# Merge stage of a three-branch mixer kernel: the LRU branch first, its first operands prepared in the stage before

## The chip, the cores and the metric

One Trainium2 chip, one core, one launch. The metric is device time in microseconds: the median of the runs of the whole kernel, about 2.9 ms.

## The reference, cut to what matters

One step of a backbone layer over 1152 tokens (128 of context, 1024 latent), width 1024, all in fp32. One input projection feeds three recurrent mixers: gated linear attention (GLA), a diagonal state space (S5) and a gated linear recurrence (LRU, width 1536). Then:

```python
ys   = gelu(s5_outputs)                                 # (T, 1024)
y_s5 = ys * sigmoid(ys @ s5_w_glu)                      # "GLU"
g_gla, g_s5, g_lru = split(sigmoid(gates), 3)
merged = (g_gla * (y_gla @ w_br_gla) + g_s5 * (y_s5 @ w_br_s5)
          + g_lru * (y_lru @ w_br_lru))
out = merged @ w_out
x = layer_norm(ALPHA * x + gate1 * out); then a squared-ReLU MLP and a second layer_norm
```

`gate1` and the other modulation vectors are silu(c) times rows of `w_ada`.

## The kernel before, in words

The program is a chain of stages. Each ends in `core.end_stage()` (line 143): the semaphores of the stage are cleared and all engines meet at a barrier. The two stages that matter are `s5_and_gates` (line 1504) and `merge_and_mlp` (line 2316).

An fp32 product is made of three TensorE passes: each operand is split in a high part (fp32r) and a low part (operand minus high part), and hi*hi, hi*lo and lo*hi are accumulated. A weight unit is 128 x 1024; it is loaded to `raw`, the high part goes to `hi`, the low part to `lo`, with two buffers of each (`Stream`, line 157). In the GLU, LRU, GLA and S5 parts of the merge GpSimd makes both parts (`Stream.split`, lines 194 and 197). A unit of activations ("tile", 128 channels x 1152 tokens) is read into one of four buffers `yin`; ScalarE copies it to a slot of `yhi` (`fill_act`, line 2478, the copy is line 2496) and VectorE subtracts to a slot of `ylo` (`fill_dve`, line 2506). There are 12 slots.

**The state-space stage.** For n = 0 to 15 (groups of 4 state-space groups) TensorE makes input products, lag blocks and outputs (`outputs`, line 1879, lines 1889 and 1891), and between them 3 or 4 "bands" of 24 matmuls of the gate projection (`band`, line 1818, line 1831). `outputs(n - 1)` comes in iteration n, so the last outputs come in iteration 16 (`LAST`), behind the last two bands. ScalarE applies the sigmoid to each band (`evac_gate`, 1981) and stores the gate tile, sets the chunk-boundary states that `outputs` waits for (`resets`, 2011 to 2015, semaphore `hn_done`), and applies gelu to the outputs (`evac_y`, 2024). SyncE, in each iteration and in this order: kernel blocks to DRAM (8 transfers, 1742 and 1744), outputs of the group before to `y_d` (8 transfers, 1753), the state weights `wia` back (8 transfers, 1761). After the loop it stores the final states (1763) and waits for all of it.

**The merge.** TensorE runs four parts in turn, with the loop `for ph in range(OUT)` at line 2666: GLU (8 output tiles m, 8 input tiles k each), LRU (8 m, 12 k), GLA (8, 8) and S5 (8, 8); for each (m, k) nine matmuls of 128x128 by 128x384 (`tile_product`, 2643, line 2662), 2592 in all. Output tile m uses banks 0 to 2 (m even) or 3 to 5 (m odd). The semaphore `used` counts (m, k) pairs, `filled` the slots filled. GLU's inputs are the tiles of `y_d`, which lie in DRAM with the time index inside the group and are turned by the strided read of both fill operations (`turned`). GLU's banks go through a sigmoid on ScalarE (2779) and two VectorE operations over a whole tile (2952, 2953), and the result is stored to `y_s5`. LRU, GLA and S5 multiply the banks by the gate tile into `x1` (`gated`, 2995, 2998, 2999). VectorE also makes 32 modulation vectors, two products each with a row of `w_ada` (`dots`, 2965): two per m in LRU, one per m in GLA and S5. There is one row buffer, so a row is loaded after the products with the row before. Slots of the next part are filled while the last tile m = 7 of the part before uses them up; on VectorE the fills stand behind the `dots` of m = 7 and before its `gated`. SyncE issues weights, gate tiles and rows in one written order (2510 to 2560).

After the four parts, `w_out`, the norms and the MLP follow (line 2695); nothing there is changed.

Of the kernel before, what the change touches and what calls it, by code (L numbers as in the profile page):

```python
# [15 lines left out]
P = 128  # L16
# [5 lines left out]
NB = 3  # L22
# [12 lines left out]
LBLK = 12  # L35
CONV = 4
# [70 lines left out]
class Early:  # L107
    COLS = 4 * T + HEADS * DK + 4 * HEADS + NPAIR + T // 2 + 2 * UW

    def __init__(self, nc, ctx):  # L110
# [9 lines left out]
        self.hi, self.lo = sb("gla_hi", [P, UW], F32R), sb("gla_lo", [P, UW], F32R)  # L120

# [1382 lines left out]
def s5_and_gates(core, hhi, hlo, lam):  # L1504

    nc, dram = core.nc, core.dram
    with ExitStack() as ctx:
# [53 lines left out]
        wt = [sb(f"wt{c}", [P, G4 * P]) for c in "ri"]  # L1561
        wtmp = sb("wtmp", [P, G4 * P])
        win = sb("win", [P, 2 * G4, P])
# [8 lines left out]
        def table_buffer(s):  # L1572
# [15 lines left out]
        kst = [sb(f"kst{s}", [P, KW]) for s in range(2)]  # L1588
        sb("kst_pad", [P, 2 * (G4 - 1) * KW])
# [4 lines left out]
         scan_done, rot_done, fin_s, hn_done, kd_out, y_out0, y_out1, fin_out, const_done) = (  # L1594
# [4 lines left out]
                "kd_out", "y_out0", "y_out1", "fin_out", "const_done"))  # L1599
# [6 lines left out]
        tab_in, y_out = [tab_in0, tab_in1], [y_out0, y_out1]  # L1606
# [38 lines left out]
        with nc.Block() as block:  # L1645
            @block.sync
            def _(sync):
# [77 lines left out]
                for n in range(LAST + 1):  # L1725
# [21 lines left out]
                    if n:  # L1747

                        sync.wait_ge(item_free, Y_ITEM[n - 1] + 1 + 1)
                        m = n - 1  # L1750
                        for t in range(SCH):
                            dst = dram["y_d"][m * G4 * S5I:(m + 1) * G4 * S5I].rearrange("(g i) t c -> i g t c", i=S5I)[:, :, t, :]
                            sync.dma_start(dst, yb[m % 2][t * S5I:(t + 1) * S5I]).then_inc(y_out[m % 2], 16)
                    if n < NBT:
# [7 lines left out]
                sync.wait_ge(fin_s, 2 * NBT)  # L1762
                sync.dma_start(dram["new_s5"], fins[:]).then_inc(fin_out, 16)
                sync.wait_ge(fin_out, 16)
                for s in range(2):
                    sync.wait_ge(y_out[s], 128 * (NBT // 2))
                    sync.wait_ge(gate_out[s], 16 * (UNITS_G // 2))

            @block.gpsimd
            def _(pool):  # L1770
# [35 lines left out]
                for n in range(LAST + 1):  # L1806
# [7 lines left out]
                    splits(bands(n, 3))  # L1814

            @block.tensor
            def _(pe):
# [61 lines left out]
                def outputs(n):  # L1879
# [4 lines left out]
                    pe.wait_ge(hn_done, 2 * n + 2)  # L1884
                    for x in range(2):
                        bk = item(Y_ITEM[n] + x)
# [6 lines left out]
                        mm.then_inc(item_done, 1)  # L1893
# [37 lines left out]
            def _(act):  # L1931
# [132 lines left out]
                for n in range(LAST + 1):  # L2064
# [16 lines left out]
                    if n:  # L2081
                        evac_y(n - 1)
                    for b in bands(n, 3):
                        evac_gate(b)

            @block.vector
            def _(dve):
# [228 lines left out]
def merge_and_mlp(core, mod, x1):  # L2316
# [6 lines left out]
    with ExitStack() as ctx:  # L2323
        ctx.callback(core.end_stage)

# [3 lines left out]
        def sem(name):  # L2329
# [4 lines left out]
        GLU, LRU, GLA_, S5_, OUT = range(5)  # L2334
        ORDER = [list(range(8)), [8, 9, 10, 11, 0, 1, 2, 3, 4, 5, 6, 7], [8, 9, 10, 11, 0, 1, 2, 3],
                 [4, 5, 6, 7, 8, 9, 10, 11], list(range(8))]
        USED = [0, 64, 160, 224, 288]
        FILL = [0, 8, 20, 28, 36]
        UNIT = [0, 8, 24, 32, 40]
        S = Stream(core, "mrg")  # L2340
        yhi = sb("yhi", [P, LBLK, T], F32R)
        ylo = sb("ylo", [P, LBLK, T], F32R)
# [44 lines left out]

        WHI = [S.hi[0][:], S.hi[1][:]] + [yhi[:, n, 0:UW] for n in (8, 9, 10, 11, 0, 1)]
# [65 lines left out]
        for ph, name, off in ((LRU, "y_lru", 1), (GLA_, "y_gla", 2), (S5_, "y_s5", 0)):  # L2454
            for k, slot in enumerate(ORDER[ph]):
                tile = slot if ph == LRU else k
                loads.append((name, tile + off, slot))
# [7 lines left out]
        free_at = ([None] * 4 + [last_use(GLU, s) for s in range(8)] + [last_use(LRU, s) for s in (8, 9, 10, 11, 0, 1, 2, 3)]  # L2465
# [866 lines left out]
```

## Time and profile before

| | |
|---|---|
| median of 3 runs | 2923.47 us (2921.84 to 2925.73) |
| the profiled execution | 2925.48 us, span 2923.6 us |
| PE busy (matmul) | 2776.7 us, 95% of the span |
| DVE, ACT, POOL busy | 1776.7, 1133.3, 939.2 us |
| mean granted clock of TensorE | 0.982 of full speed |
| state-space stage, last band of the gates begins its last matmul | 1483.34 us |
| merge, TensorE's first matmul | 1510.35 us |
| first matmul of `w_out` | 1975.03 us |

The span runs from the first to the last instruction; the execution's own time lies 1.9 us above it. PE is TensorE's matmul side, DVE VectorE, ACT ScalarE, POOL GpSimd, SP SyncE; a q behind an engine's name marks its queue, that is issued transfers, register and semaphore work. L2662 is line 2662 of the kernel. A name is cut to its stem: w_raw, w_hi and w_lo are the weight buffers. The granted clock is given as a share of 2.4 GHz: 1.00 is that, 0.50 is 1.2 GHz.

### The profile page before, as it was taken

To read this page: it belongs to the slowest core of one execution; us is meant where nothing else is said; L and a number is where in the kernel's file an instruction comes from. 1 tells how busy PE (TensorE), PEld (TensorE's weight loads), DVE (VectorE), ACT (ScalarE), POOL (GpSimd) and SP (SyncE) were. 2 spreads that over 40 slices of the span, in tenths; PEclk is the share of its full clock that TensorE was granted. 3 is DMA by queue.
4 is the path that set the end of the run, shared out by engine and by line. 5 is a ranking of instruction groups with operands and counts; after the bars stand their busy time and mean duration, and the time that the engine had idled before them with its cause. 6 is when DMAs were issued, how large, how long until landed. Compare 5 with 4: busy or idle time off the path is not lost. (4 is left out here: it accounts for less than half of the span.)

```text
span 2923.6 us, 41670 instructions
## 1 busy us (share of the span) xinstructions
PE 2776.7 (95%) x16768; PEld 2717.0 (93%) x16768; DVE 1776.7 (61%) x2422; ACT 1133.3 (39%) x1709; POOL 939.2 (32%) x624
## 2 busy tenths in 40 slices
PE   6999999999999998999969999999999999999996
PEld 6999998899999998999969999999899999999996
DVE  7678876454454899999964547778732233223226
ACT  2698995352643323444441101014632211211224
POOL 1344443111211265666523433333112212111223
PEclk9999999999999999999989999999999999999998
DMA  6111112011201444444453536344111111111111
GB/s 230 45 66 55 66 60 62 28 34 44 58 24 42 140 163 145 125 124 123 117 179 118 190 130 224 128 134 140 36 44 44 44 40 42 43 44 44 44 44 65
DMA packets 112716, 257.81 MB, mean 88 GB/s; under 512 B 22496, under 2 KB 56288, under 8 KB 112288
## 3 DMA queue, kind: packets, MB, share of 16 engines
q1 hardware_dynamic: 102464, 214.27, 23.6%
q10 hardware_dynamic: 10080, 41.18, 3.9%
q8 instruction: 117, 1.92, 0.3%
q14 instruction: 55, 0.45, 0.1%
HBM read 199.01 MB, written 56.37 MB: 87 GB/s over the span
## 5 line engine op out<-in xcount | busy, mean ns | idle before, releaser
L153 POOL TENSOR_TENSOR w_lo<-w_raw,w_hi 128x256 fp32r<-128x256 f32 x292 | 348.6, 1224 | 704.5 <-ACT w_hi L205 494.7
L2695 PE MATMUL bank<-yhi,w_hi 128*128 128x384 f32 x1560 | 525.4, 337 | 3.3 <-POOL w_lo L2625 1.8
L2695 PE MATMUL bank<-ylo,w_hi 128*128 128x384 f32 x1560 | 522.0, 335 | 0.0
L2695 PE MATMUL bank<-yhi,w_lo 128*128 128x384 f32 x1560 | 521.9, 335 | 0.0
L2625 POOL TENSOR_TENSOR w_lo<-w_raw,w_hi 128x1024 fp32r<-128x1024 f32 x69 | 169.4, 2456 | 678.4 <-ACT w_hi L2803 678.4
L2662 PE MATMUL bank<-yhi,w_hi 128*128 128x384 f32 x864 | 291.7, 338 | 29.5 <-POOL w_lo L197 24.0
L2695 PEld LDWEIGHTS bank<-yhi,w_hi 128*128 128x128 f32 x1560 | 293.6, 188 | 6.8 <-POOL w_lo L2625 2.5
L2695 PEld LDWEIGHTS bank<-ylo,w_hi 128*128 128x128 f32 x1560 | 293.6, 188 | 1.2 <-issue 0.3
L2695 PEld LDWEIGHTS bank<-yhi,w_lo 128*128 128x128 f32 x1560 | 293.5, 188 | 0.0
L2662 PE MATMUL bank<-ylo,w_hi 128*128 128x384 f32 x864 | 290.5, 336 | 0.0
L2662 PE MATMUL bank<-yhi,w_lo 128*128 128x384 f32 x864 | 290.3, 336 | 0.0
L3114 DVE SCALAR_TENSOR_TENSOR x<-bank,mod,x 128x384 f32<-128x384 f32 (+2 forms) x256 | 126.1, 515 | 242.1 <-PE bank L2695 241.8
L1831 PE MATMUL bank<-hhi,w_hi 128*128 128x384 f32 x744 | 257.9, 347 | 6.6 <-ACT gate L1965 6.6
L1831 PE MATMUL bank<-hhi,w_lo 128*128 128x384 f32 x744 | 251.3, 338 | 0.0
L1831 PE MATMUL bank<-hlo,w_hi 128*128 128x384 f32 x744 | 251.1, 337 | 0.0
L433 PE MATMUL bank<-hhi,w_hi 128*128 128x384 f32 x648 | 218.6, 337 | 13.9 <-DVE hlo L768 10.2
L3103 DVE TENSOR_TENSOR mrg_scr<-gt 128x384 f32<-128x384 f32 x96 | 53.6, 558 | 282.5 <-ACT yhi L2831 282.4
L433 PE MATMUL bank<-hlo,w_hi 128*128 128x384 f32 x648 | 218.0, 336 | 0.0
L433 PE MATMUL bank<-hhi,w_lo 128*128 128x384 f32 x648 | 218.0, 336 | 0.0
L2803 ACT ACTIVATE w_hi<-w_raw 128x1024 fp32r<-128x1024 f32 x69 | 72.6, 1052 | 324.4 <-PE bank L2695 313.6
L2662 PEld LDWEIGHTS bank<-yhi,w_hi 128*128 128x128 f32 x864 | 163.5, 189 | 32.8 <-POOL w_lo L197 24.9
L194 POOL TENSOR_TENSOR w_hi<-w_raw,zero 128x1024 fp32r<-128x1024 f32 (+1 forms) x40 | 77.7, 1943 | 273.0 <-PE bank L2662 176.9
(453 smaller groups left out, 6504.5 us busy)
## 6 DMA issues: line engine op xcount, KB each, us to landing
w_raw<-in_mlp_units SPq DMA_DIRECT2D x64, 512.0 KB, 3.6
w_raw<-in_s_units SPq DMA_DIRECT2D x32, 512.0 KB, 4.6
mrg_scr<-in_w_ada_rows SPq DMA_DIRECT2D x32, 512.0 KB, 3.7
mid_gates<-gate ACTq DMA_DIRECT2D x24, 576.0 KB, 3.6
gt<-mid_gates SPq DMA_DIRECT2D x24, 576.0 KB, 3.9
w_raw<-in_gla_units SPq DMA_DIRECT2D x25, 512.0 KB, 3.7
w_raw<-in_lru_units SPq DMA_DIRECT2D x24, 512.0 KB, 3.7
x<-in_x_t SPq DMA_DIRECT2D x16, 576.0 KB, 9.9
```

The source lines that it names most:

```text
L153: ins = pool.tensor_tensor(lo[:, part], raw[:, part], hi[:, part].bitcast(F32), ALU.subtract)
L194: pool.tensor_tensor(self.hi[par][:, w], self.raw[par][:, w], self.core.zero.to_broadcast([P, width]), ALU.add).then_inc(self.hi_done, 1)
L433: mm = pe.matmul(out, wts[u % 2][:, w], r[:, k, cols], start=(k == 0 and n == 0), stop=(k == KD - 1 and n == 2))
L1831: mm = pe.matmul(out, wts[par][:, w], r[:, k, cols], start=(k == 0 and x == 0), stop=(k == KD - 1 and x == 2))
L2625: pool.tensor_tensor(WLO[SLOT[u]], S.raw[u % 2], WHI[SLOT[u]].bitcast(F32), ALU.subtract).then_inc(S.split_done, 1)
L2662: mm = pe.matmul(out, wt[par][:, w], r[:, slot, cols], start=(k == 0 and n == 0), stop=(k == len(order) - 1 and n == 2))
L2695: mm = pe.matmul(out, wt[SLOT[u]][:, w], r[:, k, band_cols(b)], start=(k == first and y == 0), stop=(k == last and y == 2))
L2803: act.activation(WHI[SLOT[u]], S.raw[u % 2], ACT.Copy).then_inc(S.hi_done, 1)
L3103: st(dve.tensor_tensor(asq, r, r, ALU.mult))
L3114: ins = dve.scalar_tensor_tensor(x1[:, m, c0:c1], core.bank[n % 6][:, c0 - b * BW:c1 - b * BW], mod[:, 5 * KD + m, c:c + 1], x1[:, m, c0:c ...
```

## The change

The merge's order becomes LRU, GLU, GLA, S5, with new slot orders. Buffers `x1` and `yhi`/`ylo` (now one array) are laid out under `hhi`/`hlo` and are given from a class `Merge` with semaphores that live across the barrier. In the state-space stage's last two iterations, the first LRU weight unit, half of the second and two LRU tiles are loaded (the tiles into the dead buffers of the input weights), and split by ScalarE, GpSimd and VectorE; six more LRU tiles are loaded raw into `x1`. The last outputs go to banks 6 and 7, and their gelu and store come in the merge. The final states are stored from ScalarE's queue. The state weights of n = 15 are loaded before the outputs of n = 14 are stored. GLU works by bands with a bank as scratch.

```diff
@@ s5_and_gates, SyncE, iteration n
+                    if n == NBT - 1:
+                        state_weights()
+                        sync.wait_ge(S.split_done, UNITS - 2 + 3)
+                        sync.dma_start(merge.raw[0][:], dram["w_br_lru"][0][:, 0:UW]).then_inc(merge.w_in[0], 16)
+                        sync.wait_ge(item_done, T_ITEM[NBT - 1] + 1 + 1)
+                        sync.wait_ge(w_done, NBT)
+                        for k in range(Merge.LEAD):
+                            sync.dma_start(lead_raw[k], dram["y_lru"][k + 1]).then_inc(merge.y_in[k], 16)
+                        sync.wait_ge(S.split_done, UNITS - 1 + 3)
+                        sync.dma_start(merge.raw[1][:, 0:4 * P], dram["w_br_lru"][0][:, UW:UW + 4 * P]).then_inc(merge.w_in[1], 16)
+                    if n == LAST:
+                        sync.wait_ge(band_done, GATED)
+                        for k in range(Merge.LEAD, KD):
+                            sync.dma_start(merge.x1[:, k, :], dram["y_lru"][k + 1]).then_inc(merge.y_in[k], 16)
+                    elif n:
...
-                sync.wait_ge(fin_s, 2 * NBT)
-                sync.dma_start(dram["new_s5"], fins[:]).then_inc(fin_out, 16)
@@ s5_and_gates, GpSimd, behind its loop
+                pool.wait_ge(merge.w_hi, 1)
+                low_parts(pool, merge.lo[0], merge.raw[0], merge.hi[0]).then_inc(merge.w_lo, 1)
+                pool.wait_ge(merge.w_hi, 2)
+                pool.tensor_tensor(merge.lo[1][:, 0:4 * P], merge.raw[1][:, 0:4 * P], merge.hi[1][:, 0:4 * P].bitcast(F32),
+                                   ALU.subtract).then_inc(merge.w_lo, 1)
@@ s5_and_gates, ScalarE
-                    if n:
+                    if n and n < LAST:
                         evac_y(n - 1)
                     for b in bands(n, 3):
                         evac_gate(b)
+                    if n == NBT - 1:
+                        act.wait_ge(merge.w_in[0], 16)
+                        act.wait_ge(band_done, 3 + NB * (UNITS - 1))
+                        act.activation(merge.hi[0][:], merge.raw[0][:], ACT.Copy).then_inc(merge.w_hi, 1)
+                act.wait_ge(band_done, GATED)
+                for k in range(Merge.LEAD):
+                    act.wait_ge(merge.y_in[k], 16)
+                    act.activation(merge.y[:, k, 0, :], lead_raw[k], ACT.Copy).then_inc(merge.y_hi, 1)
+                act.wait_ge(merge.w_in[1], 16)
+                act.activation(merge.hi[1][:, 0:4 * P], merge.raw[1][:, 0:4 * P], ACT.Copy).then_inc(merge.w_hi, 1)
+                act.wait_ge(fin_s, 2 * NBT)
+                act.dma_start(dram["new_s5"], fins[:]).then_inc(fin_out, 16)
+                act.activation(warm[:], ident[:, 0:1], ACT.Gelu_apprx_tanh)
@@ s5_and_gates, VectorE, behind its loop
+                for k in range(Merge.LEAD):
+                    dve.wait_ge(merge.y_hi, k + 1)
+                    dve.tensor_tensor(merge.y[:, k, 1, :], lead_raw[k], merge.y[:, k, 0, :].bitcast(F32),
+                                      ALU.subtract).then_inc(merge.y_lo, 1)
@@ merge_and_mlp
-        GLU, LRU, GLA_, S5_, OUT = range(5)
+        LRU, GLU, GLA_, S5_, OUT = range(5)
@@ merge_and_mlp, SyncE
+                for f in range(KD, LBLK):
+                    sync.dma_start(yin[f % 4][:], dram["y_lru"][f + 1]).then_inc(yin_in[f % 4], 16)
                 lru_units(1)
+                tile_of("gates", 2 * KD, 0, 0)
+                tile_of("gates", 2 * KD + 1, 0, 1)
+                sync.wait_ge(merge.last_free, 2)
... (8 stores of the last outputs to y_d, then crow and bada)
+                for m in range(5, KD):
+                    lru_units(m)
+                    tile_of("gates", 2 * KD + m, m // 2, m % 2)
+                    for a in (2 * m - 9, 2 * m - 8):
+                        load_row(a, 2 * a)
+                for m in range(2):
+                    tile_unit(GLU, m, m)
+                load_row(7, 14)
+                for m in range(2, KD):
+                    tile_unit(GLU, m, m % 2)
+                    load_row(6 + m, 12 + 2 * m)
+                for m in range(2):
+                    tile_unit(GLA_, m, m)
+                    load_row(14 + m, 28 + 2 * m)
                 for s in range(2):
                     sync.wait_ge(y_out[s], 16 * (KD // 2))
+                for m in range(2):
+                    tile_of("gates", m, 4 * GLA_, m)
+                load_row(16, 32)
+                for m in range(2, KD):
+                    tile_unit(GLA_, m, m % 2)
...
@@ merge_and_mlp, ScalarE
+                act.wait_ge(merge.last_mm, 2)
+                for x in range(2):
+                    act.activation(merge.yb[:, 2 * x:2 * x + 2, :],
+                                   core.bank[LAST_BANK[x]][:, 0:2 * NCH].rearrange("p (g c) -> p g c", c=NCH),
+                                   ACT.Gelu_apprx_tanh).then_inc(merge.last_free, 1)
+                for f in range(Merge.LEAD, LBLK):
+                    fill_act(act, f)
...
+                for f in range(12, 20):
+                    fill_act(act, f)
@@ merge_and_mlp, VectorE
                 for m in range(KD):
-                    dots(2 * m)
-                    dots(2 * m + 1)
+                    if m >= 4:
+                        dots(2 * m - 8)
+                        dots(2 * m - 7)
                     if m == KD - 1:
-                        for n in range(12, 20):
-                            fill_dve(dve, n)
+                        for f in range(12, 20):
+                            fill_dve(dve, f)
                     gated(LRU, m)
```

Fills 12 to 19 are now GLU's turned tiles, 20 to 27 GLA's and 28 to 35 S5's. GpSimd's splits keep their rule (a unit is split when its buffers are free), now in the new order and from the second LRU unit on.

## Rows read from the trace of the kernel before

**Rows 1.** Waits of PE in 1480 to 1980 us: total, times, longest.
```profile
PE bank L2662 <- POOL w_lo L197: 24.0, 3, 21.5
PE bank L2662 <- DVE ylo L2506: 5.5, 7, 1.6
```

**Rows 2.** Timeline around the barrier: start us, us, engine, what, [idle before <-releaser].
```profile
1483.72 0.49 ACT L1981 ACTIVATE gate<-bank 128x384 f32<-128x384 f32 x1 [3.67 <-PE bank L1831]
1485.35 0.21 ACT L2015 ACTIVATE hn<-s_init 64x8 f32<-64x8 f32 x1
1485.66 0.48 PE L1889 MATMUL bank<-ub,wia 128*128 128x144 f32 x2 [1.98 <-DMA wia<-mid_kd]
...
1488.43 0.41 PE L1891 MATMUL bank<-hn,ca1i 128*128 128x144 f32 x2
1489.48 3.63 SPq L1753 DMA_DIRECT2D mid_y_d<-yb  x8
1493.15 0.43 SPq L1763 DMA_DIRECT2D out_new_s<-s_fins  x1
1495.95 0.10 POOL L2602 MEMSET ln_eps<- 128x1 f32 x1 [42.08 <-POOLq L146]
...
1510.35 0.69 PE L2662 MATMUL bank<-yhi,w_hi 128*128 128x384 f32 x1 [21.51 <-POOL w_lo L197]
```

**Rows 3.** Windows: stretch, us, PE, PEld, DVE, ACT, POOL busy, PEclk, DMA, GB/s.
```profile
1496.50:1509.50 13.00, 0.00 (x0) 0.00 (x0) 7.14 (x3) 7.35 (x4) 5.39 (x2) 0.50 0.98 381
1510.30:1526.50 16.20, 14.71 (x63) 13.43 (x63) 16.18 (x6) 12.34 (x7) 7.79 (x2) 0.82 0.76 240
1628.00:1660.00 32.00, 28.20 (x159) 27.16 (x158) 19.80 (x21) 2.91 (x3) 16.06 (x8) 1.00 0.64 231
1660.00:1776.00 116.00, 116.00 (x671) 116.00 (x670) 59.85 (x73) 7.02 (x6) 46.46 (x25) 1.00 0.47 155
1776.00:1804.00 28.00, 25.29 (x136) 24.64 (x135) 23.68 (x29) 5.85 (x5) 9.16 (x5) 0.94 0.69 235
```

**Rows 4.** Timeline of SP's queue, last iterations of the state-space stage.
```profile
1473.98 0.42 SPq L1744 DMA_DIRECT2D mid_kd<-kst  x1
1476.00 3.64 SPq L1753 DMA_DIRECT2D mid_y_d<-yb  x8
```

**Rows 5.** DMA issues: engine queue, count, KB each, median us to landing.
```profile
w_raw<-in_s_units SPq DMA_DIRECT2D x32, 512.0 KB, 4.6
out_new_s<-s_fins SPq DMA_DIRECT2D x1, 64.0 KB, 1.6
```

**Rows 6.** Lines of one source line each: duration in ns, min/median/max.
```profile
L1981 ACT ACT_TABLE_LOAD  x16: 1283/1283/1283, 1055.3 to 1476.0; - x16
L2496 ACT ACTIVATE yhi<-yin x36: 1154/1172/2277, 1500.1 to 1874.4; 128x1152 fp32r<-128x1152 f32 x36
L2506 DVE TENSOR_TENSOR ylo<-yin,yhi x36: 1345/1358/4292, 1502.4 to 1875.6; 128x1152 fp32r<-128x1152 f32 x36
L194 POOL TENSOR_TENSOR w_hi<-w_raw,zero x40: 1041/1894/3706, 1504.0 to 1950.0; 128x1024 fp32r<-128x1024 f32 x32, 128x512 fp32r<-128x512 f32 x8
L197 POOL TENSOR_TENSOR w_lo<-w_raw,w_hi x40: 1287/2493/4129, 1506.3 to 1951.9; 128x1024 fp32r<-128x1024 f32 x32, 128x512 fp32r<-128x512 f32 x8
```

**Rows 7.** The chain that ended last, stretch 1500 to 1800 us: start us, us, what.
```profile
1504.43 2.68 DVE ylo L2506
...
1508.05 2.69 DVE ylo L2506
...
1752.15 1.02 DVE x L2995 x2
...
1756.58 3.73 DMA mrg_scr<-in_w_ada_rows
...
1763.06 14.26 DVE ylo L2506 x5
...
1786.67 6.11 DMA w_raw<-in_w_br_gla
```

More of the change, by code:

```diff
@@ L35 @@
 LBLK = 12
+LAST_BANK = (6, 7)
 CONV = 4
@@ L2324, in merge_and_mlp @@
         ctx.callback(core.end_stage)
+        core.sems += merge.sems
         def sb(name, shape, dt=F32):
@@ L2453, in merge_and_mlp @@
         loads = []
-        for ph, name, off in ((LRU, "y_lru", 1), (GLA_, "y_gla", 2), (S5_, "y_s5", 0)):
+        for ph, name, off in ((LRU, "y_lru", 1), (GLU, "y_d", 0), (GLA_, "y_gla", 2), (S5_, "y_s5", 0)):
             for k, slot in enumerate(ORDER[ph]):
-                tile = slot if ph == LRU else k
-                loads.append((name, tile + off, slot))
+                loads.append((name, k + off, slot))
         def last_use(ph, slot):
@@ new lines, in raw_tile, with fill_act @@
+        def raw_tile(f):
+            if f < KD:
+                return x1[:, f, :]
+            return turned(yin[f % 4]) if loads[f][0] == "y_d" else yin[f % 4][:]
+        def fill_act(act, f, src=None, slot=None):
+            if src is None:
+                src, slot = raw_tile(f), loads[f][2]
+                if f >= 14:
+                    act.wait_ge(filled, f - 1)
+                    issue(act, f + 2)
+                if f < KD:
+                    act.wait_ge(merge.y_in[f], 16)
+                else:
+                    act.wait_ge(yin_in[f % 4], ring(f)[1])
+                if free_at[f] is not None:
+                    act.wait_ge(used, free_at[f])
@@ new lines, in _ @@
+                for t in range(SCH):
+                    dst = dram["y_d"][last * G4 * S5I:(last + 1) * G4 * S5I].rearrange("(g i) t c -> i g t c", i=S5I)[:, :, t, :]
+                    sync.dma_start(dst, merge.yb[t * S5I:(t + 1) * S5I]).then_inc(merge.y_out[last % 2], 16)
+                sync.wait_ge(merge.y_out[0], 128 * (NBT // 2))
+                sync.dma_start(crow, dram["crow"].rearrange("c d -> (c d)").partition_broadcast(P)).then_inc(crow_in, 16)
+                sync.dma_start(bada[:], dram["bada"][:, NMOD1:6 * KD]).then_inc(bada_in, 16)
@@ L3188, in build @@
         mod = ctx.enter_context(nc.sbuf_tensor("mod", [P, 6 * KD, 2], F32))
+        core.weight_buffers(ctx)
+        with ExitStack() as over:
+            merge = Merge(core, over)
         with ExitStack() as hctx:
@@ L3283, in layout @@
     out["s5_init"] = np.ascontiguousarray(st.transpose(1, 3, 0, 2)).reshape(P, 2, GROUPS)
-    order = [LBLK - HG + k for k in range(HG)] + list(range(LBLK - HG))
-    w = f["w_br_lru"][0].reshape(LBLK, P, D)[order].reshape(LBLK * P, D)
-    out["w_br_lru"] = units(w, slice(None))
-    for name in ("w_br_gla", "w_br_s5", "w_out"):
+    for name in ("w_br_lru", "w_br_gla", "w_br_s5", "w_out"):
         out[name] = units(f[name][0], slice(None))
```

273 lines of the change are left out of this document (138 added, 135 removed).

## The prediction

> **What bounds the kernel now.** I read the windows first. In 1660 to 1776 us, inside the LRU part, PE is busy for all of 116.00 us with 671 matmuls, 0.173 us each, at clock 1.00 [rows 3]: the merge runs at TensorE's rate, and only time in which TensorE stands still or runs slow can be won. The waits of PE say where it stands: 21.5 us in one wait for a low part of a weight unit, and 8.0 us in all the rest (2.5 for low parts, 5.5 for filled slots) [rows 1]. The timeline around the barrier shows that wait. The last band is done when its sigmoid starts, at 1483.7. PE waits 1.98 us, makes the last outputs (1485.66 to 1488.84) and then stands 21.51 us, to 1510.35 [rows 2]. In that time the outputs are stored (3.63 us of issue), the final states too, the barrier opens at 1495.95, and from 1496.5 to 1509.5 DMA runs at 381 GB/s with a share of 0.98 [rows 2, 3]: the merge has to load, split and fill before its first matmul.
>
> The merge itself loses in three stretches. A stretch's loss is its length less its matmuls by 0.173. Start, 1510.3 to 1526.5: 16.2 - 63 x 0.173 = 5.3. GLU to LRU: 32.0 - 159 x 0.173 = 4.5. LRU to GLA: 28.0 - 136 x 0.173 = 4.5 [rows 3]. With 1.98 and 21.51 that is 37.8 us which the change can touch. Matmuls, outputs and everything from `w_out` on stay as they are.
>
> **The change, part by part.**
>
> *Step 1, the wait before the last outputs.* The state weights no longer stand behind the store of outputs 14, so the transfer that ended the 1.98 us comes 3.6 us earlier. But ScalarE now has a wait for the first LRU weights in front of the last two sigmoids, and behind those stand the resets that TensorE waits for. SyncE issues the last kernel block by 1474.4 [rows 4]. I put its landing 2 us later (between the 1.6 and 4.6 of [rows 5], nearer the small transfer), then 8 transfers at the pace of the y store, 3.64 us [rows 4]: 1480.0. A 512 KB unit lands 4.6 us after issue in this stage [rows 5]: 1484.6. Then ScalarE makes the high part, about 1.04 us (a 1152-column copy takes 1.17 [rows 6], scaled), and reloads the sigmoid table, 1.28 [rows 6], which the idle time hides today. The first sigmoid begins at 1486.9, the last at 1487.4. From the start of the last sigmoid to the end of the last reset it is 1.84 us [rows 2]: 1489.3. TensorE starts its outputs at 1489.4, 5.7 us after the last band instead of 1.98, and ends them at 1492.6. Bounds: 2 (the weights land before ScalarE is there) to 9 (they come 3 us later, behind gate and state traffic). TensorE's last bands are not held up, since their banks are freed by the bands before.
>
> The Trainium skill's page ScalarE: Activation LUTs, section What ACT_TABLE_LOAD costs, says that a drain of about 1.38 us comes on top of a load of 1283 ns. The row agrees with the load; with that drain in series step 1 would be 7.1 us instead of 5.7.
>
> *Step 2, from the outputs to the merge's first matmul.* Behind the resets ScalarE copies two tiles (2 x 1.17), the half unit (0.5) and issues the final states (0.43): 1492.6. VectorE's two subtractions (1.36 each [rows 6]) and GpSimd's low parts (2.5 and 1.3) end by about 1494. The final states took 1.6 us to land [rows 5], but now six raw tiles of 576 KB, issued from 1485.5 on, are in the DMA engines: 3.5 MB at 381 GB/s is 9 us, to 1495. I take 2.4 us, and for the barrier the 0.77 between landing (1493.58 + 1.6) and 1495.95 [rows 2]. The merge opens at 1495.8, about when it does today: the 4 us saved on the y store go to the new chain. TensorE then needs only the counts that SyncE sets; SyncE's loads today reach full rate 0.55 us behind the barrier [rows 2, 3], so 0.6 us: first matmul 1496.4 instead of 1510.35. The idle is 3.8 us in place of 21.5. Bounds 2.5 (states land in 1.6, no other traffic) and 8 (4.6 for them, and gate stores late).
>
> *Step 3, the start.* Two tiles are ready, 18 matmuls. The clock of 0.82 over 16.2 us is 2.9 us lost at the 1.2 GHz level [rows 3]; the idle is shorter, but [rows 3] also show 0.94 over 28 us (1.7 us) around a wait of only some 2 us, so I keep 2.9 (bounds 0 and 5.3, all of today's loss). Meanwhile ScalarE evacuates the last outputs (0.7, an estimate for twice 288 columns at the rate of [rows 6]) and fills at 1.17 and 1.36 us per tile, faster than the nine matmuls' 1.56. The third tile is ready 3.5 us after the opening, TensorE wants it after 6: no wait. Tiles 9 to 12 are loaded by then. GpSimd's first unit is due 12 us later. The y store, `crow` and `bada` have the length of three LRU tiles. Loss 3.2 with small change, for 5.3.
>
> *Step 4, LRU to GLU.* In time from the start T of LRU's m = 7 (today about 1751.3, its `gated` for m = 6 is at 1752 [rows 7]): VectorE does two `dots`, the row between is issued at T + 5.3 and lands 3.7 later, and its fills begin at T + 11.8 [rows 7]. This does not change. But the eight fills are now the turned ones. Behind them GpSimd splits the next unit from T + 12.5. Today's turned fills beside such a split took 2.7 us each and came every 3.6 us (1504.43, 1508.05) [rows 7]; unturned fills take 1.36 [rows 6]. Starting at T + 11.8: tile 1 at 14, tile 5 at about 28.5, where TensorE wants it at T + 18.7 + 6.2 = 24.9; after that at 2.1 us a tile (an estimate between 1.36 and 2.7) against 1.56, another 1.5. And the unit's split, 3.7 + 4.1 at worst [rows 6], ends at T + 20.3 for a need at 18.7. These overlap in part: I take 5.5, with bounds 2 (fills every 2.7) and 10 (all eight at 3.6 and the banks of m = 7, freed behind them, late as well).
>
> The Trainium skill's GPSIMD Engine Reference, section on specifications, has GpSimd's memory interfaces shared with VectorE, with contention where a VectorE instruction has two operands in SBUF. The fills are of that kind, and the rows agree: 1.36 grows to 2.7 and GpSimd's 1.89 to 3.7. Without such a rule step 4 would cost 2.
>
> *Step 5, GLU to GLA.* The gate tiles wait for the last store of y_s5, which waits for VectorE's fills and its banded products: sigmoids to 1.5 us after GLU's end (0.49 each [rows 2]), four fills and two products over 1152 columns at 1.36 with the hops between them to 11.5, store landed at 15 (3.6, and 4.5 for a load, estimates below the 4.6 of [rows 5]), gate tile at 19.5, row and `dots` at 22, `gated` of m = 0 done at 26; TensorE wants the banks at 25. Behind the same wait stands the third GLA unit: issued at 17, 6.1 us as today [rows 7], split 4.4 to 6: 27 to 29 for 25. That is the place of today's 1786.67 load. With fills 24 to 27 beside a split (1 us) and one drop of the clock as today (1.7, part of the time) I take 4.5, today's loss for such a change-over [rows 3]. Bounds 1 and 8. GLA to S5 lost nothing today, and its row, now one step later in SyncE's order, still comes some 9 us ahead: 0. GLU in the middle: two products, one `dots` (two of 1024 columns) and one fill are some 7 us of VectorE in 12.5, at 1.36 for 1152 columns.
>
> **Sum.** 5.7 + 3.8 + 3.2 + 5.5 + 4.5 = 22.7 us for 37.8: 15 us less. The profiled execution would take 2925.5 - 15 = 2910.5; it lies 2.0 above the median of 2923.5, so the median becomes 2908.5.
>
> **Rivals.** (a) *A new wait eats more*: the LRU weights land late, or the final states land behind the raw tiles, steps 1 and 2 at their upper bounds (9 and 8). That adds 7.5: 2916. For it: DMA at 0.98 in the start today, and everything that waits is in one line on ScalarE. Against: the weights are the first large transfer. Chance 0.17. (b) *The change-overs are clean*: steps 4 and 5 at 2 and 1, with half of step 3's clock loss: 8.5 less, 2900. For it: S5's change-over loses nothing. Against: [rows 7]. 0.15. (c) *The transfer is hidden anyway or the change gives nothing*: the new merge opens so late (about 1509) that the loads happen before the barrier rather than behind it, 2923. It needs final states or gate store to take over 14 us; no row has that in this stage. 0.05. (d) *Slower: TensorE falls to 1.2 GHz and stays there*, in the first GLU tile, where four or more short waits follow one another. A matmul at half the clock costs up to 0.173 more. The gain is used up at 87 such matmuls, and the kernel is slower by over 0.2% from 121, a fifth of GLU: 2933 with 140. Against: [rows 3] show 0.94 over 28 us, ten matmuls or so, behind such waits. 0.03. The Trainium skill's page TensorE: Matmul & The Clock Gate, section HAM oscillation, describes such a kernel, throttled again in each gap between short bursts; the windows show it for single gaps only.
>
> **Chances.** The forecast itself 0.60. The range that leaves out 2 in 10 goes from 2899, where (b) lies, to 2918, above (a). 0.2%, about what a measurement of this kernel can tell from no change, is 5.8 us. Only (c), part of the edge of (a), and (d) are not faster by that: faster 0.92, same 0.05, slower 0.03.
>
> **What would show it.** Right: PE's wait before the last outputs near 5.7, ended by ScalarE; the merge's first matmul near 1496 with an idle of about 4 us before it; no wait for filled slots in LRU's m = 0; waits of 4 to 7 us in all at GLU's first tile, ended by `ylo`; a wait near 2 us at GLA's third tile, ended by GpSimd's low part behind a weight load. Wrong: an idle over 8 us at the barrier; waits in the LRU part; a granted clock under 0.9 over a whole part; any change behind the first matmul of `w_out` beyond the shift.

## The result, and the profile after

| | before | after |
|---|---|---|
| median | 2923.76 us (2921.84 to 2925.73, 4 runs) | 2950.7 us (2947.49 to 2951.61, 4 runs) |
| the profiled execution | 2925.48 us, span 2923.6 us | 2951.5 us, span 2949.7 us |
| mean granted clock of TensorE | 0.982 | 0.979 |
| merge, first matmul | 1510.35 us | 1499.09 us |
| first matmul of `w_out` | 1975.03 us | 2000.19 us |

The ratio is 1.0086 [1.0074, 1.0098]: 27 us slower, where I had forecast 15 us faster. The first two marks of the merge divide it. It begins 11.3 us earlier (14.0 were forecast), and from its first matmul to the first of `w_out` it takes 501.1 us in place of 464.7: 36.4 us more, where 1.1 were forecast to be saved (37.8 less 22.7 in all, 14.0 of it ahead of the merge). Net 25.2 of the 26.1 us of the span.

The waits of PE over the whole span, of the changed kernel: engine and tile, line, releaser, total us, times, longest (the waits of other stages left out). They answer to [rows 1].

```profile
PE bank L2772 <- DVE x L3087: 21.0, 11, 11.6
...
PE bank L2772 <- DVE mrg_y L2593: 9.1, 7, 4.1
...
PE bank L2805 <- issue: 7.0, 1, 7.0
...
PE bank L1947 <- issue: 4.6, 1, 4.6
PE bank L2772 <- SPq L2600: 4.6, 1, 4.6
...
PE bank L2772 <- POOL w_lo L228: 0.9, 1, 0.9
```

The 21.5 us wait for a low part is gone. In its place stand 4.6 us before the last outputs (L1947), 4.6 before the merge's first matmul (L2772 behind SyncE's counts), 9.1 for filled slots, and 21.0 us in eleven waits for `gated` (L3087), which no row of before had. One of those is 11.6 us long; the other ten share 9.4 and look harmless. The windows say that they are not. Columns as in [rows 3]:

```profile
1483.50:1497.50 14.00, 6.41 (x30) 5.91 (x29) 2.63 (x2) 8.29 (x13) 4.90 (x5) 0.74 1.02 369
1497.50:1514.00 16.50, 14.91 (x73) 14.94 (x74) 12.78 (x10) 11.24 (x12) 0.10 (x1) 0.81 0.98 370
1514.00:1640.00 126.00, 126.00 (x729) 126.00 (x728) 31.68 (x49) 7.61 (x4) 46.38 (x28) 1.00 0.38 127
1640.00:1700.00 60.00, 54.70 (x306) 52.41 (x305) 53.80 (x46) 21.43 (x19) 26.15 (x8) 1.00 0.54 181
1756.00:1805.00 49.00, 37.36 (x201) 37.07 (x200) 28.31 (x29) 10.27 (x11) 11.97 (x6) 0.86 0.54 200
1805.00:1990.00 185.00, 170.78 (x952) 166.75 (x951) 120.89 (x143) 11.68 (x10) 66.93 (x25) 0.98 0.33 117
1990.00:2010.00 20.00, 12.96 (x61) 12.67 (x60) 18.29 (x22) 6.09 (x6) 7.45 (x4) 0.74 0.62 232
```

The LRU part from 1514 to 1640 is full: 729 matmuls in 126 us, no wait, as forecast. With 0.173 us a matmul, LRU to GLU loses 60 - 306 x 0.173 = 7.1, GLU to GLA 49 - 201 x 0.173 = 14.2, the rest of GLA and S5 185 - 952 x 0.173 = 20.3 and S5 to `w_out` 9.4. The same two last stretches of the kernel before, behind the change-over that [rows 3] end at 1804, are nearly full:

```profile
1804.00:1967.00 163.00, 163.00 (x942) 163.00 (x941) 119.13 (x142) 12.87 (x11) 59.39 (x25) 1.00 0.44 145
1967.00:1987.00 20.00, 18.81 (x106) 17.87 (x105) 18.21 (x23) 6.98 (x8) 8.74 (x5) 1.00 0.56 191
```

They lose nothing and 1.7. So 28.0 us, more than three quarters of the 36.4, come from GLA, S5 and the passage to `w_out`, to which I gave nothing.

What happens there is read from the chain that ended last, here of the changed kernel between 1925 and 1940 us: start us, us, what.

```profile
1925.69 0.33 SPq L2607
...
1926.07 4.52 DMA mrg_scr<-in_w_ada_rows
...
1930.61 1.30 DVE bank L3053 x2
...
1933.27 0.57 DVE gt L3086
...
1933.86 1.47 DVE x L3087
1935.33 0.48 DVE gt L3086
...
1935.83 2.17 DVE x L3087
...
1938.51 0.57 DVE x L3087
...
1939.10 0.33 SPq L2607
...
1939.47 4.81 DMA mrg_scr<-in_w_ada_rows
```

TensorE isn't in it at all. It is a closed loop: SyncE issues a gate tile (L2607, it waits until the `gated` of two tiles ago has freed the buffer), behind it in the written order the row of `w_ada` (4.52 us to land), VectorE makes the `dots` with it (two products, to 1933.24), then `gated` (5.8 us from 1933.27 to 1939.08), which frees the next gate buffer. From row to row it is 1939.47 - 1926.07 = 13.40 us; TensorE needs 72 x 0.173 = 12.5 us for the same output tile. So the loop, not TensorE, sets the pace, about 0.9 us a tile. In the kernel before, a row was for the `dots` of its own tile, so the same chain of waits had two tiles' time, 25 us, to close.

### The profile page after: what moved, and what is told of

Its sections match the earlier page's. It is cut to its first block and busy times, and to the rows that moved or that the text cites. A ratio compares the mean times of both kernels' runs of the same rounds, so it can differ in the third digit from the quotient of the medians.

```text
span 2949.7 us, 41400 instructions
## 1 busy us (share of the span) xinstructions
PE 2788.3 (95%) x16768; PEld 2725.5 (92%) x16768; DVE 1770.8 (60%) x2454; ACT 1133.5 (38%) x1712; POOL 934.0 (32%) x625
## 5 line engine op out<-in xcount | busy, mean ns | idle before, releaser
L2805 PE MATMUL bank<-mrg_y,w_hi 128*128 128x384 f32 x3120 | 798.1, 336 | 10.0 <-issue 7.0
L2805 PEld LDWEIGHTS bank<-mrg_y,w_hi 128*128 128x128 f32 x3120 | 565.7, 189 | 14.4 <-issue 7.9
L2805 PE MATMUL bank<-mrg_y,w_lo 128*128 128x384 f32 x1560 | 522.6, 335 | 0.0
L2772 PE MATMUL bank<-mrg_y,w_hi 128*128 128x384 f32 x1728 | 446.6, 339 | 35.7 <-DVE x L3087 21.0
L2772 PEld LDWEIGHTS bank<-mrg_y,w_hi 128*128 128x128 f32 x1728 | 315.3, 190 | 42.8 <-issue 24.6
L2805 PEld LDWEIGHTS bank<-mrg_y,w_lo 128*128 128x128 f32 x1560 | 294.2, 189 | 0.0
L2772 PE MATMUL bank<-mrg_y,w_lo 128*128 128x384 f32 x864 | 291.7, 338 | 0.0
L2772 PEld LDWEIGHTS bank<-mrg_y,w_lo 128*128 128x128 f32 x864 | 164.6, 190 | 0.0
L1887 PEld LDWEIGHTS bank<-hhi,w_hi 128*128 128x128 f32 x744 | 141.5, 190 | 13.6 <-issue 13.2
L1887 PEld LDWEIGHTS bank<-hlo,w_hi 128*128 128x128 f32 x744 | 141.5, 190 | 0.0
## 6 DMA issues: line engine op xcount, KB each, us to landing
x<-in_x_t SPq DMA_DIRECT2D x16, 576.0 KB, 10.4
```

Source lines behind the costliest of these rows:

```text
L1887: mm = pe.matmul(out, wts[par][:, w], r[:, k, cols], start=(k == 0 and x == 0), stop=(k == KD - 1 and x == 2))
L2772: mm = pe.matmul(out, wt[par][:, w], r[:, slot, cols], start=(k == 0 and n == 0), stop=(k == len(order) - 1 and n == 2))
L2805: mm = pe.matmul(out, wt[SLOT[u]][:, w], r[:, k, band_cols(b)], start=(k == first and y == 0), stop=(k == last and y == 2))
```

## The experiments

Theory A: the row's place in SyncE's order, behind the wait for a gate tile, has made a serial loop, and this is the larger part of the 27 us. Theory B: the change-overs (slow fills beside GpSimd's splits, loads behind the wait for the y_s5 stores) are, and the loop's waits only follow them. All kernels below compute the whole reference. Experiments 1 to 4 ran on one chip, where the kernel before took 2923.15 us (median of 19 runs), and 5 to 8 on another, where it took 2925.76 (8 runs, 2920.43 to 2932.57); every ratio below is to the kernel before on the same chip. In the recorded expectations e4, e8, e9 and e10 stand for experiments 4, 5, 6 and 7.

**1. The row ahead of the gate tile.** The changed kernel with two lines exchanged, in GLA for m from 2 and in S5:

```diff
                     tile_unit(GLA_, m, m % 2)
-                    tile_of("gates", m, 4 * GLA_ + m // 2, m % 2)
                     load_row(15 + m, 30 + 2 * m)
+                    tile_of("gates", m, 4 * GLA_ + m // 2, m % 2)
... (the same two lines exchanged in S5)
```

> The changed kernel with two lines of SyncE swapped in the GLA and S5 parts: the row of the modulation weights is loaded ahead of the gate tile instead of behind it. Theory A (a serial loop): the gate tile waits for gated of m - 2, the row waits behind it, dots wait for the row and gated of m - 1 for dots, so gate wait, row 4.7, dots 2.6 and gated 4.2 us make a loop of 13.5 us against TensorE's 12.5. With the row ahead of the wait the loop falls under 12.5: PE's waits for L3087 after the first one (9.4 us in 10 waits) vanish, so do the 4.8 at S5's first fills and most of the 7.0 before w_out; total 15 to 22 us less, 2929 to 2936. Theory B (VectorE's operations are lengthened by GpSimd's splits beside them, the order does not matter): the period stays near 13.5 and the total at 2951.

Measured: 2923.8 us (2921.69 to 2924.47), ratio to before 0.9998 [0.9988, 1.0008], 26.9 us less than the changed kernel. SyncE's queue and the two windows, of this kernel:

```profile
1916.84 0.33 SPq L2607 DMA_DIRECT2D gt<-mid_gates  x1
1917.21 0.43 SPq L213 DMA_DIRECT2D w_raw<-in_w_br_s  x1
1922.03 0.33 SPq L2620 DMA_DIRECT2D mrg_scr<-in_w_ada_rows  x1
1929.33 0.33 SPq L2607 DMA_DIRECT2D gt<-mid_gates  x1
```

```profile
1805.00:1990.00 185.00, 183.80 (x1057) 182.86 (x1056) 142.74 (x162) 20.81 (x22) 67.32 (x31) 1.00 0.43 151
1990.00:2010.00 20.00, 20.00 (x118) 20.00 (x117) 19.59 (x18) 7.04 (x15) 8.32 (x4) 1.00 0.51 176
```

The row now goes out 7.3 us before the next gate tile instead of 0.4 behind it, the period is 12.49 us, which is TensorE's, and the two windows lose 2.1 us and nothing (185 - 1057 x 0.173) in place of 29.7. A is right: VectorE's additions in `gated` are still slowed here (1.70 and 2.17 us, at 1923.86 and 1926.07, beside GpSimd's split), and the pace is TensorE's all the same. My figure was too small, since I went by the waits of this stretch, at most 21.2 us (9.4 for `gated`, 4.8 for slots, 7.0 before `w_out`). PE's idle in the two windows of the changed kernel is just that, 14.2 + 7.0; the other 8.5 of the 29.7 is in its busy time, 170.78 us for 952 matmuls and 12.96 for 61 where 0.173 each gives 164.7 and 10.6, at clocks of 0.98 and 0.74 where experiment 1 has 1.00 in both: behind its waits TensorE ran part of the time at the lower level.

**2. The same in the kernel before.** The other way round: there, rows of GLA and S5 come one step later and behind the next gate tile; nothing else is changed.

```diff
-                    with sync.Fori(0, 4) as i:
...
-                            tile_of(src, t0 + 2 * i + j, 4 * ph + i, j)
-                            load_row(a0 + 2 * i + j, 2 * a0 + 4 * i + 2 * j)
+                    for m in range(KD):
...
+                        tile_of(src, t0 + m, 4 * ph + m // 2, m % 2)
+                        if a0 + m > 2 * KD:
+                            load_row(a0 + m - 1, 2 * (a0 + m - 1))
+                load_row(4 * KD - 1, 2 * (4 * KD - 1))
```

> The kernel before the change with only SyncE's order in GLA and S5 altered: each row is loaded one step later, behind the next gate tile, as in the changed kernel. Theory A: the same serial loop of 13.5 us arises without anything else of the change, 1 us for each of some 14 tiles, and the last row comes late for w_out: 15 to 25 us more, 2938 to 2948. Theory B (contention or the new order of parts is the cause): under 3 us more.

Measured: 2954.43 us (2951.43 to 2956.43), 1.0106 [1.0089, 1.0122]: 31.3 us slower than before. Waits of PE, 1480 to 2010 us:

```profile
PE bank L2663 <- DVE x L3000: 11.6, 12, 3.3
PE bank L2663 <- DVE ylo L2506: 10.5, 9, 4.2
PE bank L2696 <- issue: 6.9, 1, 6.9
```

SyncE's queue in this kernel, two rows of the loop:

```profile
1914.57 0.43 SPq L2530 DMA_DIRECT2D mrg_scr<-in_w_ada_rows  x1
...
1928.02 0.43 SPq L2530 DMA_DIRECT2D mrg_scr<-in_w_ada_rows  x1
```

The period is 13.45 us, and there are the same three waits as after the change: many short ones for `gated`, slots filled late, 6.9 us before `w_out`. The place of the rows in SyncE's order alone costs the old kernel more than the whole change cost, with the old merge order and the old barrier. Again I had priced it too low.

**3. Only the row behind the y_s5 stores.** The changed kernel with row 16 issued ahead of SyncE's wait for the last y_s5 stores, behind which it had stood:

```diff
+                load_row(16, 32)
                 for s in range(2):
                     sync.wait_ge(y_out[s], 16 * (KD // 2))
                 for m in range(2):
                     tile_of("gates", m, 4 * GLA_, m)
-                load_row(16, 32)
```

> The changed kernel with only the load of row 16 moved ahead of SyncE's wait for the stores of y_s5. In the changed kernel this row is issued at 1776.00 behind two gate tiles, beside five y_s5 tiles, and takes 10.65 us, and PE then waits 11.6 us for gated of GLA's m = 0. Theory A: the row was the last to come; now the first gate tile is (5.9 us after 1775.15), gated starts near 1781.5 and ends near 1787, PE's wait falls to about 4 us, and as the later loop of 13.5 us only follows, the total falls by 5 to 8: 2943 to 2946. Rival: the DMA engines are full from 1775 to 1788 (385 to 415 GB/s) whichever transfer is first, the third weight unit then ends the wait, and the total falls by under 2.

Measured: 2940.12 us (2939.88 to 2942.07), 1.0054 [1.0037, 1.0071], 10.6 less than the changed kernel, where I expected 5 to 8. The chain of the changed kernel shows what the row cost in its old place:

```profile
1771.93 3.15 DMA mid_y_s<-gt
...
1776.00 10.65 DMA mrg_scr<-in_w_ada_rows
...
1786.67 1.30 DVE bank L3053 x2
```

The row took 10.65 us, where the loop's rows take 4.5 to 4.8, as five tiles of y_s5 (7.7 us in the median), two gate tiles and a weight unit (12.3 us) were in the DMA engines too. With it ahead, the 11.6 us wait goes, and another comes: PE waits 7.3 us for the low part of the third GLA unit, which still stands behind the y_s5 wait. The loop's waits stay (7.3 in nine). So B has a part too, the 11 us wait which experiment 1 left standing and which the early row takes down by a third or so, no more, while the next load behind the same wait is late.

**4. Both, and the fills first.** Experiments 1 and 3 together, and at LRU's m = 7 the eight GLU fills stand between the two `dots`, so that they don't wait for the second row:

```diff
                     if m >= 4:
                         dots(2 * m - 8)
-                        dots(2 * m - 7)
                     if m == KD - 1:
                         for f in range(12, 20):
                             fill_dve(dve, f)
+                    if m >= 4:
+                        dots(2 * m - 7)
```

> The changed kernel with the edits of the two runs before it on the changed kernel, and VectorE's fills of GLU's tiles ahead of the second dots of LRU's m = 7. Theory A: 15 to 22 from the order of rows, 5 to 8 from row 16, and about 5 of the 9 us lost in GLU's first tile, whose fills today begin only after the row between the dots has come: 25 to 33 less, 2918 to 2926, at or just under the kernel before, with the 11 us won at the barrier kept. If the fills are slow by the splits beside them alone, the third part is missing: 2923 to 2931.

Measured: 2916.38 us (2913.65 to 2920.02), 0.9974 [0.9965, 0.9984]. That is 34.3 less than the changed kernel, just beyond the 25 to 33 expected, and 6.8 less than the kernel before: now the change is worth something. Waits of PE, 1480 to 2010 us, first lines:

```profile
PE bank L2772 <- POOL w_lo L228: 9.4, 2, 7.8
PE bank L2772 <- SPq L2600: 5.4, 1, 5.4
PE bank L1947 <- issue: 4.8, 1, 4.8
```

No wait for a filled slot of the four parts is left. The 7.8 us wait is for the third GLA unit, as in experiment 3. LRU to GLU and GLU to GLA in this kernel:

```profile
1640.00:1700.00 60.00, 57.05 (x328) 56.44 (x327) 54.86 (x50) 21.45 (x19) 26.55 (x9) 1.00 0.59 195
1756.00:1805.00 49.00, 41.22 (x223) 40.90 (x222) 35.86 (x40) 9.72 (x10) 14.70 (x7) 0.90 0.64 233
```

They lose 3.3 us (60 - 328 x 0.173) in place of 7.1 and 10.4 (49 - 223 x 0.173) in place of 14.2: 7.6 together, which is what this kernel gains over experiment 1 (7.4). The gains don't add up, then: alone, the early row was worth 10.6, here it and the early fills together give 7.4.

**5. The third unit too.** Experiment 4 with that load ahead of the y_s5 wait, behind row 16:

```diff
                 load_row(16, 32)
+                tile_unit(GLA_, 2, 0)
                 for s in range(2):
                     sync.wait_ge(y_out[s], 16 * (KD // 2))
...
                 for m in range(2, KD):
-                    tile_unit(GLA_, m, m % 2)
+                    if m > 2:
+                        tile_unit(GLA_, m, m % 2)
```

> The kernel of e4 with the load of GLA's third weight unit ahead of SyncE's wait for the stores of y_s5. In e4 PE still waits 7.8 us at GLA's third tile, ended by the unit's low part, because SyncE issues the load at 1772.62 behind that wait and two gate tiles. Theory A: the wait falls to that of gated for m = 0, between 0 and 4 us, and with it most of the slow clock behind it (2.9 us): 5 to 10 less than e4, 2906 to 2911. Rival: the gate tiles and gated were just behind the unit; then under 3 less.

Measured: 2911.42 us (2909.2 to 2912.13), 0.995 [0.9935, 0.9965]. That is 5.0 less than experiment 4 by the medians, which are of two chips, and 14.3 below its own kernel before where experiment 4 was 6.8 below: 5.0 to 7.6, in the range of theory A. The wait for the low part falls to 1.6, and 4.1 for a `gated` in that change-over come up in its place.

**6. ScalarE's copy behind the sigmoids.** Experiment 5, and in the state-space stage the high part of the first LRU unit is made behind the last two sigmoids and the resets:

```diff
-                    if n == NBT - 1:
-                        act.wait_ge(merge.w_in[0], 16)
-                        act.wait_ge(band_done, 3 + NB * (UNITS - 1))
-                        act.activation(merge.hi[0][:], merge.raw[0][:], ACT.Copy).then_inc(merge.w_hi, 1)
                 act.wait_ge(band_done, GATED)
+                act.wait_ge(merge.w_in[0], 16)
+                act.activation(merge.hi[0][:], merge.raw[0][:], ACT.Copy).then_inc(merge.w_hi, 1)
```

> The kernel of e8 with ScalarE's copy of the first LRU weights behind the last sigmoids and resets instead of in front of them. Theory A: the wait before the last outputs falls from 4.8 to about 2 us (resets alone), the outputs come at full clock (3 us instead of 5), but the barrier opens no earlier, since SyncE waits for the gate store and the final states, which lie behind the raw LRU tiles in the DMA engines: the gate store is issued some 3 us earlier, so at best 0 to 3 us less than e8. Rival: TensorE's late outputs hold the barrier: 4 to 5 less.

Measured: 2908.46 us (2906.9 to 2911.3), 0.994 [0.992, 0.996]. The wait before the outputs falls from 4.1 to 2.0 us, and they run at full rate. The profiled spans, 2909.5 and 2909.8, and the intervals don't tell 5 and 6 apart in total. These two are the fastest found: 0.5 to 0.6% below the kernel before and, by the ratios, 1.3 to 1.4% below the changed one.

**7 and 8. Fewer raw tiles ahead of the barrier.** Two of the six raw LRU tiles are issued before the barrier and four behind it, in experiment 6's kernel (7) and in the changed kernel alone (8):

```diff
-                        for k in range(Merge.LEAD, KD):
+                        for k in range(Merge.LEAD, 4):
                             sync.dma_start(merge.x1[:, k, :], dram["y_lru"][k + 1]).then_inc(merge.y_in[k], 16)
...
+                for k in range(4, KD):
+                    sync.dma_start(x1[:, k, :], dram["y_lru"][k + 1]).then_inc(merge.y_in[k], 16)
                 for f in range(KD, LBLK):
```

> The kernel of e9 with only two of the six raw LRU tiles loaded ahead of the barrier and four behind it. 2.4 MB less stand beside the gate store and the final states. Theory A (these transfers set the barrier): they land by 1492 to 1493, the merge's first matmul comes 3 to 5 us earlier than in e9, tile 4 is filled before TensorE wants it, total 3 to 5 less. Rival: the barrier is set by ScalarE's, VectorE's and GpSimd's own work (their last ends near 1494 in the changed kernel) or the tiles come too late behind it: within 1.5 us of e9.

> The changed kernel with only the edit of e10: two raw tiles ahead of the barrier, four behind it. It says at what time the gate store and the final states land and when the barrier opens when 2.4 MB less are in flight: near 1495 instead of 1498.65 by theory A, 1498 or later if they do not set it. The total says little beside the loop of 13.5 us behind it: 2947 to 2951.

Measured: 2910.17 us (2908.61 to 2913.37), 0.9946 [0.9926, 0.9966] for 7, and 2948.16 (2946.61 to 2949.7), 1.0077 [1.0051, 1.0104] for 8. The barrier opens sooner, as the mark behind it shows, first of experiment 6, then of 7 (timeline of POOL):

```profile
1497.28 0.10 POOL L2717 MEMSET ln_eps<- 128x1 f32 x1 [2.38 <-POOLq L177]
```

```profile
1495.31 0.10 POOL L2719 MEMSET ln_eps<- 128x1 f32 x1 [1.13 <-POOLq L177]
```

Of these 2.0 us, 0.8 come from ahead of the edit: TensorE was through with the last band at 1485.65 in 6 and at 1484.89 in 7, and from there the barrier took 11.6 and 10.4 us. The rest isn't in the total, which is the same within its interval. ScalarE then waits up to 1.6 us for a tile that comes behind the barrier, and PE 2.0 us in LRU for a low part. In 8 the barrier opens at 1497.05 instead of 1498.65, 11.4 us behind the last band instead of 14.1: SyncE waits 7.7 us for the gate store and no longer for the final states. That is neither the 1495 of theory A nor the 1498 of the other; the raw tiles were part of what held the barrier. A miss for 7; 8 gained 2.5 us by the medians, of two runs and with an interval that holds the changed kernel's ratio, so a gain in total isn't shown.

## Why the prediction was wrong, point by point

**The step that failed** is the end of step 5: "GLA to S5 lost nothing today, and its row, now one step later in SyncE's order, still comes some 9 us ahead: 0". I took the distance of today's row and subtracted a step without drawing what then stands in front of it. One step later, the row for the `dots` of m - 1 stands behind the wait for gate buffer m, which the `gated` of m - 2 ends; `dots` and `gated` of m - 1 come behind the row on VectorE. With today's order the row is for a `dots` one tile further on, and the ring has two tiles' time. Its length could have been estimated from parts that I had: row 3.73 [rows 7] and an issue of 0.4, two products of 1024 columns and six operations over 384 columns at the rate of [rows 6] (2.4 and 2.7) are some 9.2 us, and 10.6 if the additions take twice as long, as the fills do beside a split. That is still under TensorE's 12.5; measured were 4.5 for the row, 2.6 for the `dots` and 5.8 for `gated`. So the rows alone wouldn't have given the loss, but they give a ring of nearly a tile's time, and that is a reason to price it, not to write 0. Experiment 1 puts the row in front of that wait and takes 26.9 us off; experiment 2 puts this order alone into the kernel before and costs 31.3.

**Step 1, the wait before the outputs.** Forecast 5.7, measured 4.6 and then 2.2 more, because the outputs ran slow. Timeline of the changed kernel: start us, us, engine, what, [idle before <-releaser].

```profile
1484.48 1.06 ACT L2146 ACTIVATE w_hi<-w_raw 128x1024 fp32r<-128x1024 f32 x1 [7.65 <-DMA w_raw<-in_w_br_lru]
1485.56 1.28 ACT L2039 ACT_TABLE_LOAD   x1
...
1486.85 0.87 ACT L2039 ACTIVATE gate<-bank 128x384 f32<-128x384 f32 x2
1487.75 0.33 ACTq L2044 DMA_DIRECT2D mid_gates<-gate  x1
...
1488.76 0.37 ACTq L2154 DMA_DIRECT2D out_new_s<-s_fins  x1
...
1489.16 0.82 PE L1947 MATMUL bank<-ub,wia 128*128 128x144 f32 x2 [4.62 <-issue]
...
1498.65 0.10 POOL L2717 MEMSET ln_eps<- 128x1 f32 x1 [4.62 <-POOLq L177]
...
1499.09 0.98 PE L2772 MATMUL bank<-mrg_y,w_hi 128*128 128x384 f32 x2 [4.56 <-SPq L2600]
```

The chain is the one forecast, nearly to the tenth: weights landed at 1484.5 (1484.6), sigmoid at 1486.85 (1486.9), outputs at 1489.2 (1489.4). Of the drain of about 1.38 us which the Trainium skill's page ScalarE: Activation LUTs, section What ACT_TABLE_LOAD costs, puts on top of a table load, these rows show nothing: the load begins 0.02 us behind the end of the copy and takes 1.28, and the sigmoid begins 0.01 behind it. The measurement decides; the 5.7, not the 7.1, was the right working. What I missed: the outputs take 5.4 us (1489.16 to 1494.54) in place of 3.2. Up to 1493.6 their pairs of matmuls follow one another every 0.48 us, in experiment 6, where the wait before them was 2.0, every 0.245: half the speed, the 1.2 GHz level. The granted clock (PEclk, the third number from the end), first of the changed kernel, then of experiment 6:

```profile
1489.10:1493.60 4.50, 4.44 (x18) 4.47 (x19) 2.63 (x2) 4.21 (x5) 1.70 (x1) 0.50 1.01 337
```

```profile
1487.60:1490.80 3.20, 3.18 (x24) 2.98 (x24) 1.12 (x1) 3.20 (x4) 2.12 (x3) 1.00 1.09 378
```

**Step 2, to the first matmul.** Forecast 3.8, measured 4.6, behind outputs that ended 1.9 us later than thought: the first matmul comes at 1499.09 instead of 1496.4. SyncE waited 6.7 us for the gate store and 1.5 for the final states. The store, 576 KB, took 8.1 us to land and the states, 64 KB, 8.7, in place of the 1.6 of [rows 5]; I had taken 2.4. It was masked in part by an error the other way: I let the states go out behind ScalarE's copies at 1492.6, but its queue issued them at 1488.76, ahead of copies that stand before them in the program. The mechanism is rival (a)'s, the amount far below its bounds: 11.4 us for steps 1 and 2 with the slow outputs, 9.5 forecast, 17 at the bounds.

**Step 3, the start.** Forecast 3.2, measured 2.3 (14.9 us from the first matmul to 1514, 73 matmuls). No wait for a slot or for weights in LRU's first tile: right.

**Step 4, LRU to GLU.** Forecast 5.5, measured 7.1, inside the bounds. VectorE and POOL in the changed kernel:

```profile
1644.04 19.95 DVE L2593 TENSOR_TENSOR mrg_y<-yin,mrg_y 128x1152 fp32r<-128x1152 f32 x6
1664.61 4.27 DVE L2593 TENSOR_TENSOR mrg_y<-yin,mrg_y 128x1152 fp32r<-128x1152 f32 x2 [0.61 <-ACT mrg_y L2584]
```

```profile
1645.16 2.80 POOL L225 TENSOR_TENSOR w_hi<-w_raw,zero 128x1024 fp32r<-128x1024 f32 x1 [10.01 <-PE bank L2772]
1648.03 4.11 POOL L228 TENSOR_TENSOR w_lo<-w_raw,w_hi 128x1024 fp32r<-128x1024 f32 x1
```

Six fills take 3.3 us each beside the splits (1.36 alone [rows 6]), and a split takes 6.9 us. The contention that the Trainium skill's GPSIMD Engine Reference, section Specifications, states for a VectorE instruction with two inputs in SBUF agrees with these rows. The term came out 1.6 too small, and I had reckoned with the split of one unit beside the fills where GpSimd split two in a row, to 1660. Experiment 4 issues the fills earlier; its waits for filled slots are gone, and the stretch loses 3.3 in place of 7.1.

**Step 5, GLU to GLA.** Forecast 4.5, measured 14.2, beyond its bound of 8. The places were right (the row and the third unit behind the y_s5 stores, `gated` of m = 0). Counted from GLU's end, 1758.8 (PE's long wait begins at 1783.7, 144 matmuls later), the last store landed 16.3 us behind it, and I had 15. The failed term is the row: its `dots` should have been done at 22 and `gated` at 26; they were at 30.5 and 36.3 (1789.3, 1795.1), since the row took 10.65 us. The bulk of the stretch, y_s5 tiles, gate tiles and weights, was in the DMA engines with it, as the raw tiles had been with the final states in step 2: the same error twice.

**The passage to `w_out`.** I held it unchanged. But the last row is at the end of the same loop: its `dots` end at 1997.5, GpSimd may not clear that buffer before, its next splits start at 1997.74, and PE waits 7.04 us. With the loop open (experiment 1) it waits 1.1.

**The balance.** Against before, 12.1 us were won at the barrier (23.5 of idle and wait became 4.6 + 2.2 + 4.6) and 3.0 in the start; 2.6 lost in LRU to GLU (7.1 for 4.5), 9.7 in GLU to GLA (14.2 for 4.5) and 28.0 behind it. That is 25.2 lost in all; the span says 26.1. What is left, about 1 us, is within what such a reading can tell: a matmul across the edge of a window is counted in both windows, which hides up to 0.2 us at each edge. None is missing: both traces have 2592 from the merge's first matmul to the first of `w_out`.

**The rivals.** (a) held in part (above); (b) didn't, as steps 4 and 5 lost 7.1 and 14.2; (c) didn't, as the merge began at 1499. The only rival on the slower side, (d), was a slow clock over a fifth of GLU; the clock is 1.00 from 1640 to 1700, where GLU begins, and from 1700 to 1756, with 324 matmuls in 56 us. The right one on that side would have been a loop on VectorE and SyncE, which I had in hand as "one step later". With the loop and the change-over mended, experiment 6 measures 2908.46 for a forecast of 2908.5. That the numbers are equal is chance: it ran on the other chip, where it is 17.3 us below the kernel before (11.7 to 23.4 by the interval) and not 15; its waits differ (2.0 + 6.9 us in steps 1 and 2, 4.0 for `gated`); and it has five edits that the forecast design had not. It shows that a gain of the size I took the change to give is there to be had, and not that my sum for it was right.

## What to carry to other kernels

When a load moves by one step in a queue that waits in written order, write down the ring it now stands in (which wait is in front of it, who ends that wait, and whether that one waits for the load) and add up its length against the period of the engine that should bound the stage; a ring 7% longer than the period, with the late slots and the late last row that it brings, cost 27 us here, and its own ten waits sum to only 9.4. Read a stretch's loss from its matmul count, not from the list of waits. And give a small transfer that something waits for the landing time of the traffic that is queued in front of it, not the one it has alone; better, issue it first, ahead of any wait that it doesn't need.

## What the runs showed of the hardware that I had not expected

- A 64 KB transfer landed in 8.7 us behind 3.5 MB of raw tiles and a gate store, against 1.6 alone [rows 5]; a 576 KB gate store in 8.1, against a median of 3.8; a 512 KB row in 10.65 us, against 3.73 [rows 7] and 4.5 in the loop.
- VectorE's addition over 384 columns with both operands in SBUF took 0.56 us alone and 1.47 and 2.17 beside GpSimd's split, all three in one `gated` of the chain above (the split ran from 1932.0 to 1937.6). Its products, which read a bank, kept their 0.56. Without these 2.5 us the ring would be 10.9 us long by this sum, an estimate, under TensorE's 12.5; no run took the contention away alone. In the kernel before the split fell on the `dots` instead: two products of 1024 columns took 2.92 and 3.25 us (1905.90, 1908.92) in place of 1.23.
- After a wait of 4.6 us the small matmuls of the last outputs ran at the 1.2 GHz level for the next 4 us. After waits of 3.9 and 4.1 (experiments 1 and 5) the first three pairs ran at full rate and the next six or seven at half; after 3.5 (experiment 3) and 2.0 (experiment 6) all ran at full rate.
- A transfer at the end of ScalarE's program was issued 0.3 us before the first of the copies that stand ahead of it there (1488.76 and 1489.08), and in experiment 6 between the two (1489.46, copies at 1488.50 and 1489.56).
- A sigmoid starts 0.01 us behind its table load of 1.28 us.
